# Two blocks of transformer layers on one core: gate and up products with the high and low activations as one 512-column operand, summed outside PSUM

## The reference, cut to what matters

```python
    # block 1
    g, u = jnp.split(x @ w_gu, 2, axis=-1)
    ffn = (jax.nn.silu(g) * u) @ w_down
    # block 2
    u = x @ w_up
    u = lax.conv_general_dilated(u, conv_w[:, None, :].astype(u.dtype), window_strides=(1,),
                                 padding=[(CONV_W - 1, 0)], ..., feature_group_count=C) + conv_b
    a, g = jnp.split(u, 2, axis=-1)
    return (a * jax.nn.silu(g)) @ w_down
```

## Time and profile before

| | |
|---|---|
| median of 3 runs | 1692.33 us |
| the profiled execution | 1695.47 us, span 1693.5 us |
| busy: PE, DVE, ACT, POOL | 1557.0, 1077.9, 745.6, 62.2 us |
| chain that ended last: PE, DVE | 70%, 16% of the span |
| FFN stages, about | 200 to 386, 557 to 742, 1031 to 1224, 1492 to 1680 us |

### The profile page before, as it was taken

One profiled execution on the slowest core, in us unless ns is written; L12 is line 12 of the kernel. 1 busy time (PEld: TensorE's weight loads), 2 busy tenths in 40 slices (PEclk: granted clock), 3 DMA queues, 4 the chain that ended last, 5 costly groups with the idle time before them and its releaser, 6 DMA issues.

```text
span 1693.5 us, 24777 instructions
## 1 busy us (share of the span) xinstructions
PE 1557.0 (92%) x10085; PEld 1412.8 (83%) x10085; DVE 1077.9 (64%) x1654; ACT 745.6 (44%) x1058; POOL 62.2 (4%) x58
## 2 busy tenths in 40 slices
PE   6789999999789999989899888999998998989997
PEld 5678899998787999968888778999887888789996
DVE  6885965567857755575454546767764545566767
ACT  4454433344553433423564234455445643344442
POOL 0200000000100000011000000000010000000000
PEclk9889999999899999999799999999998998999999
DMA  8513555655324665643414534556435146245551
GB/s 290 176 66 111 198 176 197 197 193 183 105 77 150 214 218 181 216 158 116 155 63 136 176 99 155 193 178 220 151 123 171 63 137 197 90 162 193 180 190 59
DMA packets 184692, 267.29 MB, mean 158 GB/s; under 512 B 7382, under 2 KB 139396, under 8 KB 184452
## 3 DMA queue, kind: packets, MB, share of 16 engines
q1 hardware_dynamic: 179684, 260.48, 46.5%
q10 hardware_dynamic: 4896, 5.25, 0.9%
HBM read 260.46 MB, written 5.24 MB: 157 GB/s over the span
## 4 chain that ended last, share of the span: by engine, by line
PE 70%; DVE 16%; DVEq 4%; ACT 3%; issue 2%; POOL 2%; DMA 2%; SPq 0%; ACTq 0%; POOLq 0%
PE psw L678 15%; PE psw L680 15%; PE psw L679 15%; PE psa L678 5%; PE psa L679 5%; PE psa L680 5%; DVE wlo L1488 4%; PE psa L815 2%; POOL rstd L2128 2%; PE psw L798 2%; DVE xtok L1520 1%; PE psw L1056 1%; DVE sy L1576 1%; DVE r L1862 1%; DMA sy<-in_xa_wq 1%
## 5 line engine op out<-in xcount | busy, mean ns | idle before, releaser
L1488 DVE TENSOR_TENSOR wlo<-raw,whi 128x2048 fp32r<-128x2048 f32 (+2 forms) x217 | 489.6, 2262 | 289.1 <-ACT whi L1165 288.4
L1165 ACT ACTIVATE whi<-raw 128x2048 fp32r<-128x2048 f32 (+2 forms) x217 | 410.0, 1891 | 335.1 <-PE psw L680 243.2
L678 PE MATMUL psw<-xhi,whi 128*128 128x256 f32 x1472 | 416.8, 283 | 2.6 <-ACT r L1346 1.4
L680 PE MATMUL psw<-xhi,wlo 128*128 128x256 f32 x1472 | 416.5, 283 | 0.0
L679 PE MATMUL psw<-xlo,whi 128*128 128x256 f32 x1472 | 416.5, 283 | 0.0
L678 PEld LDWEIGHTS psw<-xhi,whi 128*128 128x128 f32 x1472 | 282.4, 192 | 5.1 <-ACT r L1346 2.2
L679 PEld LDWEIGHTS psw<-xlo,whi 128*128 128x128 f32 x1472 | 282.4, 192 | 1.3
L680 PEld LDWEIGHTS psw<-xhi,wlo 128*128 128x128 f32 x1472 | 282.4, 192 | 0.0
L678 PE MATMUL psw<-whi,xhi 128*128 128x512 f32 (+3 forms) x472 | 185.3, 393 | 22.0 <-DVE wlo L1488 16.9
L679 PE MATMUL psw<-wlo,xhi 128*128 128x512 f32 (+3 forms) x472 | 181.8, 385 | 0.0
L680 PE MATMUL psw<-whi,xlo 128*128 128x512 f32 (+3 forms) x472 | 181.8, 385 | 0.0
(11 more groups left out here) (274 smaller groups left out, 2194.4 us busy)
## 6 DMA issues: line engine op xcount, KB each, us to landing
raw<-in_w_gu SPq DMA_DIRECT2D x44, 1024.0 KB, 5.1
raw<-in_ffn_w_up SPq DMA_DIRECT2D x42, 1024.0 KB, 5.1
raw<-in_w_down SPq DMA_DIRECT2D x22, 1024.0 KB, 5.1
raw<-in_ffn_w_down SPq DMA_DIRECT2D x22, 1024.0 KB, 4.9
raw<-in_w_in SPq DMA_DIRECT2D x20, 1024.0 KB, 5.4
raw<-in_xa_wkv SPq DMA_DIRECT2D x16, 1024.0 KB, 5.6
raw<-in_w_o SPq DMA_DIRECT2D x8, 1024.0 KB, 5.2
raw<-in_w_out SPq DMA_DIRECT2D x8, 1024.0 KB, 5.2
```

The source lines that it names most:

```text
L678: pe.matmul(o, lh, rh, start=first, stop=False)
L680: return pe.matmul(o, ll, rh, start=False, stop=last)
L1165: nc.scalar.activation(tile_flat("hi", i), tile_flat("raw", i), ACT.Copy).then_inc(hi_ready, 1)
L1488: v.tensor_tensor(tile_flat("lo", i), tile_flat("raw", i), tile_flat("hi", i).bitcast(F32), ALU.subtract).then_inc(lo_ready, 1)
```

## The change

Activations high and low lie side by side (xboth). For gate and up of all four FFNs the high weights multiply both at once, one matmul of 512 columns: its first 256 columns go to the high half of a PSUM bank, the others to the low half. The low weights' matmul of 256 columns adds to the high half. So a half of 128 features fills a bank, a gate tile banks 0 and 1, an up tile banks 2 and 3, and there is no second set. ScalarE copies the low halves out (`ffn_low`), VectorE adds the high halves to them (`ffn_sum`), and SiLU, Identities, taps and products read the sums gsum and usum in SBUF. TensorE takes a bank again when ffn_summed says so. In block 2 the taps of gate and of up are two groups of four, and SiLU stands in front of up's part. The last two down tiles are taken token half by token half.

The diff, cut:

```diff
-        xhi = sb("xhi", [KD, S], F32R)
-        xlo = sb("xlo", [KD, S], F32R)
+        xboth = sb("xboth", [2, KD, S], F32R)
+        xhi, xlo = xboth[:, 0], xboth[:, 1]
...
+        gsum = r2[:, 0:512]
+        usum = r2[:, 512:1024]
+        low_part = r2[:, 1024:2048].rearrange("p (i c s) -> p i c s", i=2, c=2)
...
+            def by_features_wide(key, bank0, free, ready=None):
+
+                wh, wl = take(key)
+                for ch in range(TC // P):
+                    bank = psw[:, bank0 + ch, :]
+                    cols = slice(ch * P, (ch + 1) * P)
+                    free(bank0 + ch)
+                    for k in range(KD):
+                        if ready is not None and ch == 0:
+                            turns_ready(ready, NT - 1, k)
+                        if k:
+                            pe.matmul(bank[:, 0:S], wl[:, k, cols], xhi[:, k, :], start=False, stop=False)
+                        ins = pe.matmul(bank.rearrange("p (i s) -> p i s", i=2), wh[:, k, cols], xboth[:, :, k, :],
+                                        start=k == 0, stop=k == KD - 1)
+                        if k == 0:
+                            pe.matmul(bank[:, 0:S], wl[:, k, cols], xhi[:, k, :], start=False, stop=False)
+                ins.then_inc(tile_done, 1)
...
-                    if f >= 2:
-                        pe.wait_ge(hid_ready, f - 1)
-                    by_features((block, "g", l, s), bank2(psw, 2 * (f % 2)), xhi, xlo,
-                                norm_key if s == 0 else None)
-                    by_features((block, "u", l, s), bank2(psw, 2 * (f % 2) + 1), xhi, xlo)
+
+                    def gate_free(bank):
+                        if s:
+                            pe.wait_ge(ffn_summed, 2 * f - 1)
+                        else:
+                            first_free(bank)
+
+                    def up_free(bank):
+                        if s:
+                            pe.wait_ge(ffn_summed, 2 * f)
+                        else:
+                            first_free(bank)
+                    by_features_wide((block, "g", l, s), 0, gate_free, norm_key if s == 0 else None)
+                    by_features_wide((block, "u", l, s), 2, up_free)
...
                 for t in range(NT):
                     for half in range(2):
                         ins = down(FS - 2, t, half)
-                        if t == 1 and half == 1:
-                            ins.then_inc(tile_done, 1)
+                    if t == 1:
+                        ins.then_inc(tile_done, 1)
+                    for half in range(2):
                         ins = down(FS - 1, t, half)
...
-                pe.wait_ge(pg_exp, 4 * (l + 1))
...
+                def gate_read(bank):
+                    pe.wait_ge(pg_exp, 4 * l + (1, 3, 2, 4)[bank])
...
+            def ffn_low(block, l, s, i):
+
+                act.wait_ge(tile_done, ti[(block, "gu"[i], l, s)] + 1)
+                nc.scalar.activation(low_part[:, i], psw[:, 2 * i:2 * i + 2, S:2 * S], ACT.Copy).then_inc(low_out, 1)
...
+                        ffn_low(1, l, s, 0)
                         serve((1, "g", l, s))
                         if f >= 2:
                             act.wait_ge(hid_ready, f - 1)
-                        act.wait_ge(tile_done, ti[(1, "g", l, s)] + 1)
-                        nc.scalar.activation(gact[:, f % 2, :], psw[:, 2 * (f % 2), :],
-                                             ACT.Silu).then_inc(gate_ready, 1)
+                        act.wait_ge(ffn_summed, 2 * f + 1)
+                        nc.scalar.activation(gact[:, f % 2, :], gsum, ACT.Silu).then_inc(gate_ready, 1)
+                        ffn_low(1, l, s, 1)
                         serve((1, "u", l, s))
...
-                            act.wait_ge(tile_done, ti[(2, name, l, s)] + 1)
+                            ffn_low(2, l, s, i)
+                            act.wait_ge(ffn_summed, 2 * f + i + 1)
                             if f >= 2:
                                 act.wait_ge(hid_ready, f - 1)
...
-                        act.wait_ge(conv_done, FS * l + s + 1)
-                        nc.scalar.activation(gact[:, f % 2, :], conv_g[:, f % 2].rearrange("p c s -> p (c s)"),
-                                             ACT.Silu).then_inc(gate_ready, 1)
+                            if name == "g":
+                                act.wait_ge(conv_done, FS * l + s + 1)
+                                nc.scalar.activation(gact[:, f % 2, :], conv_g[:, f % 2].rearrange("p c s -> p (c s)"),
+                                                     ACT.Silu).then_inc(gate_ready, 1)
...
+            def ffn_sum(block, l, s, i):
+
+                dve.wait_ge(low_out, 2 * (FS * (l + L * (block - 1)) + s) + i + 1)
+                v.tensor_tensor((gsum, usum)[i].rearrange("p (c s) -> p c s", c=2), psw[:, 2 * i:2 * i + 2, 0:S],
+                                low_part[:, i], ALU.add).then_inc(ffn_summed, 1)
...
+                def taps(l, s, i, buf, whole, ch0):
+
+                    f = FS * (L + l) + s
+                    dve.wait_ge(conv_first, 2 * (FS * l + s) + i + 1)
+                    for tap, lag in ((1, 1), (0, 2)):
+                        for ch in range(2):
+                            cc = 44 * tap + ch0 + ch
+                            o = buf[:, f % 2, ch, lag:S]
+                            ins = v.scalar_tensor_tensor(out=o, in0=whole[:, ch * S:(ch + 1) * S - lag],
+                                                         scalar=pcol[:, 1 + 2 * l, cc:cc + 1], in1=o, op0=ALU.mult,
+                                                         op1=ALU.add)
+                        if tap:
+                            dve.drain()
+                    return ins
...
+                        ffn_sum(2, l, s, 0)
                         serve((2, "g", l, s))
...
+                        taps(l, s, 0, conv_g, gsum, 22 + 2 * s).then_inc(conv_done, 1)
+                        ffn_sum(2, l, s, 1)
                         if s < FS - 1:
                             serve((2, "u", l, s))
+                        taps(l, s, 1, conv_a, usum, 2 * s)
                         dve.wait_ge(gate_ready, f + 1)
```

More of the change, by code:

```diff
@@ L406, in build @@
         xpT_ready = sem("xpT_ready")
+        low_out = sem("low_out")
+        ffn_summed = sem("ffn_summed")
         conv_first = sem("conv_first")
@@ L833, in attention, with ffn @@
                                 ins.then_inc(pt_done, 1)
-            def ffn(block, l, f0, norm_key, behind_up=lambda: None):
+            def ffn(block, l, f0, norm_key, behind_up=lambda: None, first_free=lambda bank: None):
                 def down(j, t, half):
@@ L970, in _ @@
                 token_stage(1, "pg", l, 4, (1, "1", l), 3, 0, before={(2, 0): lambda: norm_turns((1, "1", l), 1)})
-                pe.wait_ge(pg_exp, 4 * (l + 1))
                 def next_p():
-                    pe.wait_ge(hid_ready, FS * (l + 1) - 1)
-                    p_turns(l + 1, 2 * ((l + 1) * FS % 2))
+                    pe.wait_ge(ffn_summed, 2 * FS * (l + 1) - 1)
+                    p_turns(l + 1, 0)
+                def gate_read(bank):
+                    pe.wait_ge(pg_exp, 4 * l + (1, 3, 2, 4)[bank])
                 if l + 1 < L:
-                    ffn(1, l, FS * l, None, next_p)
+                    ffn(1, l, FS * l, None, next_p, gate_read)
                 else:
-                    ffn(1, l, FS * l, None)
+                    ffn(1, l, FS * l, None, first_free=gate_read)
             for l in range(L):
@@ L1452, in _ @@
                     if s < FS:
-                        for name, buf, bank, ch0 in (("g", conv_g, 2 * (f % 2), 22 + 2 * s),
-                                                     ("u", conv_a, 2 * (f % 2) + 1, 2 * s)):
-                            act.wait_ge(tile_done, ti[(2, name, l, s)] + 1)
+                        for i, (name, buf, whole, ch0) in enumerate((("g", conv_g, gsum, 22 + 2 * s),
+                                                                     ("u", conv_a, usum, 2 * s))):
+                            ffn_low(2, l, s, i)
+                            act.wait_ge(ffn_summed, 2 * f + i + 1)
                             if f >= 2:
@@ L1460, in _ @@
                                 cc = ch0 + ch
-                                ins = nc.scalar.activation(buf[:, f % 2, ch, :], bank2(psw, bank)[:, ch, :],
+                                ins = nc.scalar.activation(buf[:, f % 2, ch, :], whole[:, ch * S:(ch + 1) * S],
                                                            ACT.Identity, scale=pcol[:, 2 + 2 * l, cc:cc + 1],
@@ L1873, in _ @@
                     if s < FS:
+                        ffn_sum(1, l, s, 0)
                         serve((1, "g", l, s))
+                        ffn_sum(1, l, s, 1)
                         if s < FS - 1:
@@ L1877, in _ @@
                         dve.wait_ge(gate_ready, f + 1)
-                        dve.wait_ge(tile_done, ti[(1, "u", l, s)] + 1)
                         dve.drain()
```

(9 more changed lines are left out.)

2 lines of the change are left out of this document (1 added, 1 removed).

## The result

The changed kernel takes **1777.0 us** (median of four runs, 1775.5 to 1779.2) against 1691.8 before: a ratio of 1.0507 (95% interval 1.0494 to 1.0521), 85 us more. The forecast was 1768 us, with a range of 1752 to 1788. The profiled execution has a span of 1777.4 us, 83.9 more than before.

A forecast was written before the change was run, and what follows sets the result against it. It took TensorE to bound the kernel before, and a VectorE-ScalarE chain block 2's FFNs after. From 1695.5 us profiled, +81 for block 2 and -5 for block 1 gave 1771.5, or 1768 as median; range 1752 to 1788.

The forecast's parts named there:

- The loop: Block 2's FFN steps: VectorE and ScalarE, both in order, close a chain of period 20.55 us whatever TensorE does.
- Its terms: Links of block 2's chain: sum with hop 0.72, Identities 1.00, ScalarE split 1.91, VectorE split 2.20, further taps and hidden.
- The taps' source: Block 2's taps reading SBUF instead of PSUM: four priced at half the old 3.38 us, plus 0.05 for a drain.
- Rival 2: Block 2's taps get shorter reading SBUF, 0.065 us off each, eight a step: 1758 us; chance 3%.
- A layer of block 2: Added time of block 2's FFN, starts and ends included: +41.6 us in layer 0, +39.4 in layer 1.
- Block 1: SiLU FFNs, TensorE-paced: 4.0 us saved a layer, less 0.6 and 0.8 at the start; two layers -5 us.
- The clock: Block 2: low clock may follow each wait before up, but the wait shrinks by as much; the period stays.
- Rival 3: Block 2: clock stays low for all of up each time, TensorE needs 21.4 us a step: 1786 us; chance 6%.
- rival 4: Gate and up matmuls: the 512-column operand in two runs gains nothing: 1776 us; chance 8%.
- The sum: Whole kernel: profiled 1695.5 us, +81 for block 2, -5 for block 1, 1771.5; less 3.1 to the median, 1768.

The follow-up runs named there:

- e1: Changed kernel with ScalarE's SiLU in block 2 moved back behind the split that follows up's Identities: 1753.8 us.
- e2: Changed kernel with each group of four taps in block 2 put ahead of the VectorE split it stood behind: 1687.2 us.
- e3: Changed kernel with the gate's sum done twice in block 2 (0.69 us and a drain of 0.08, 22 times): 1791.4 us.
- e9: Changed kernel with the 512-column matmul taken apart into two of 256 columns: 1783.8 us.
- e6: e2's kernel with the last of four sigmoid pieces in block 1 moved behind the first sums on VectorE: 1680.5 us.
- e10: e2's kernel with the 512-column matmul taken apart into two of 256 columns: 1698.9 us.
- e4: e2's kernel with the gate's sum done twice in block 2 (0.77 us, 22 times): 1700.9 us.

## Why the prediction was right

**The loop, right.** It said that VectorE and ScalarE close a chain with a period of 20.55 us whatever TensorE does. Measured 20.72. e1, e2, e3 and e9 show each side of it: take 1.2 us out of the chain and the period falls by 1.28; overlap taps and ScalarE's split and the chain falls to 15.98, under TensorE's step; add 0.77 and it is 0.77 longer; add to TensorE and it doesn't move.

**Its terms.** Sum to Identities 0.72, Identities to split 1.00, ScalarE's split 1.93: all as said, the Identities from SBUF by the estimate included. The term that was mis-sized is the taps with their drain, from the start of a group of four to what follows it: 1.86 and 1.90 us where the sums had 1.77 and 1.82. That is 0.17 a period, and the whole difference. The two taps on either side of a drain start 0.55 us apart, the others 0.40, so a drain costs some 0.15, and I had given a group 0.05 on top of its half of the old one.

**The taps' source.** They read SBUF now and are no shorter: 479 ns on average in the profile's page against 475. Rival 2, and with it the difference that the Trainium skill, "VectorE: DVE Perf Modes", section "The TRN2 errata", gives between the two sources on VectorE, is not seen in these operations. On ScalarE it is: an Identity went from 560 to 594 ns, in the direction that the Trainium skill gives there.

**A layer of block 2, 41.6 and 39.4 said, 44.1 and 44.1 measured.** In layer 0 the loop's 0.17, over nine steps, is 1.5 of the 2.5 us. From up's last sum to the release of the last down tile I had 7.8 us; it took 8.4 (1239.97 to 1248.38), 0.35 of it between the cast and the difference. The clock then stayed low for eleven matmuls, not eight, 0.7 us, and step 0 was 0.3 shorter than said. The wait there was 8.2 us; the prediction says only that it would be longer than 2.7, and its 8.2 us are the matmuls behind it. For layer 1 I had also taken layer 0's time before. To its last down matmul layer 1 was 2.0 us shorter then (190.9 against 192.9), mostly because its clock didn't fall behind the same wait of 2.7 us; that is 2.0 of the 4.7, and the rest I didn't take apart.

**Block 1, -5 said, -2 measured.** The step is 16.63 instead of 16.58, and both starts had a stretch at the low clock, where I had taken half its price. That gate 1 would wait 2.7 us for the sum of gate 0 was right to the tenth, and e6 took it away.

**The clock, right.** Granted clock of a stretch ahead of a wait of 3.0 us, of the wait, and of up's start (busy by engine, clock, DMA):

```profile
1126.00:1137.50 11.50, 11.22 (x56) 9.01 (x55) 6.87 (x8) 4.39 (x6) 0.00 (x0) 1.00 0.52 171
1137.50:1142.40 4.90, 1.89 (x11) 1.39 (x9) 2.34 (x2) 4.80 (x5) 0.00 (x0) 1.00 0.41 131
1142.40:1146.00 3.60, 3.59 (x15) 3.12 (x16) 3.30 (x7) 0.00 (x0) 0.00 (x0) 0.71 0.38 152
```

The clock did fall in many steps (37 us of that FFN at the low level, 8 before), and the wait took it up: the prediction said 3.2 us in front of each up, and there were 3.0 where the clock had stayed up and 2.2 where it had fallen in the step before. Rival 3 didn't come, and rival 4, an operand in two runs without gain, fell with e9 and e10.

**The sum.** +88.2 for block 2, -2.0 for block 1, -2.3 elsewhere: +83.9 in the profiles. The 8 us between the 76 of the forecast and that are block 2's layers (7) and block 1 (3), less the 2 elsewhere, which nothing in the forecast stands for.

## What to carry to other kernels

Where two in-order engines hand work back and forth, write down one step as a chain, with the program order of both as links, and see whether it closes; its length is a floor for the step, and neither engine's busy share tells it. What stands between a result and its first reader in an engine's order is paid in full in such a chain: work that nobody waits for soon (here the weight splits) belongs behind work that the other engine waits for. And an engine that is freed of work gains only as far as the next chain: 0.35 us a step were to be had, 3.7 were lost, and two lines in another order brought both back in the steady step. In the whole kernel they brought less, 5 us under the kernel before: a chain just under the pace of the slowest engine has little room to catch up what the first step put it behind, and e4 shows what 0.77 us more then cost.

## What the runs showed of the hardware

A 512-column moving operand in two runs of 256 from different places costs as much as one in one piece, to 0.03 us a tile: a gate tile of 16 such and 16 of 256 columns took half of 16.63 - 5.46, 5.59 us, against 5.56 by the starts in the earlier trace rows.

How long the low clock lasts behind a wait of TensorE doesn't follow the wait's length in these traces. Behind 2.7 us it was eight matmuls of 512 columns in block 2's first FFN before and none behind the same wait in the second (starts 0.31 us apart, then 0.23, from 1674.6 us on). Behind 5.2 us it was thirteen in e2, behind 8.2 us eleven in the changed kernel, 0.43 us apart.

The same code between block 1's and block 2's FFNs took 274.9 or 280.9 us in different profiles, with 50 or 56 us at the low clock. In this program, differences of less than some 6 us between two single profiles say little unless the stretch that differs is the one that was edited.
